# Placing the large on-chip arrays at multiples of 512 bytes in a two-layer backbone kernel

## What is computed

```
def sq_relu_mlp(h, w1, w2):
    return jnp.square(jax.nn.relu(h @ w1)) @ w2

for l in range(DEPTH):                       # 2 layers
    mod_x = (jax.nn.silu(c) @ w_mod[l] + b_mod[l])[:, None, :]
    ...
    hx = rms_norm(xs, norm_mix_g[l]) * (1 + sc1) + sh1
    oc, ox = even_mixer(...) if l % 2 == 0 else odd_mixer(...)
    xs = xs + g1 * ox
    xs = xs + g2 * sq_relu_mlp(rms_norm(xs, norm_mlp_g[l]) * (1 + sc2) + sh2, mlp_w1[l], mlp_w2[l])
    ...
return rms_norm(xs, final_norm_g)            # (1, 256, 1024)
```

## The kernel before, in words

| array | before | after |
|---|---|---|
| `cst` (constants: `ident`, `ones`, masks) | 128 (`le` and behind: 160) | the same |
| `vec` | 288 | 288 |
| `cs` | 128 | 128 |
| `xT`, `raw`, `w_hi`, `w_lo` | 128 | 0 |
| `w_hi2`, `w_lo2`, `late_w` | 64 | 0 |
| all of `F`: `h_*`, `hid_*`, `mix_*`, `att_*`, `qkv`, `first_w`, `d_*` | 64 | 0 |
| row k of `up_hi`, `up_lo` | 64 (k + 1) | 64 k |

## Time and profile before

### The profile page before, as it was taken

The page is one execution under the profiler, slowest core; times in us unless marked ns, Lnnn a source line. Parts: engine busy times, 40 slices in busy tenths (PEclk is TensorE's granted clock), DMA queues, the critical chain, the costliest instruction groups (busy, mean ns, idle before and its releaser), DMA issues.

```text
span 1369.7 us, 28118 instructions
## 1 busy us (share of the span) xinstructions
PE 1344.8 (98%) x11256; PEld 1269.9 (93%) x11256; DVE 854.4 (62%) x1308; ACT 701.6 (51%) x1135; POOL 287.9 (21%) x296
## 2 busy tenths in 40 slices
PE   6999999999999999999999999999999999999998
PEld 4899998988899999999999999999998988999998
DVE  4755789985455665543587666566736666765563
ACT  4468888878544455422533322333226665663553
POOL 2000224223566786621100000000020000200002
PEclk9999999999999999999999999999999999999999
DMA  9732232322401110123466565565423320656562
GB/s 327 201 87 85 79 92 78 94 78 77 139 33 34 61 33 32 63 78 101 139 193 193 184 194 190 185 192 182 134 93 123 98 74 32 192 175 204 173 194 78
DMA packets 138030, 170.88 MB, mean 125 GB/s; under 512 B 10912, under 2 KB 121760, under 8 KB 137920
## 3 DMA queue, kind: packets, MB, share of 16 engines
q1 hardware_dynamic: 137312, 169.13, 39.4%
q0 software_dynamic: 608, 0.19, 0.1%
HBM read 168.25 MB, written 1.05 MB: 124 GB/s over the span
## 4 chain that ended last, share of the span: by engine, by line
PE 84%; DVE 7%; ACT 4%; issue 2%; POOL 2%; DMA 1%; SPq 0%; DVEq 0%; ACTq 0%; POOLq 0%
PE bank L2531 54%; PE bank L2538 7%; PE bank L2945 3%; PE bank L2933 3%; DVE qkv L1721 2%; DVE w_lo L1655 2%; PE bank L2457 1%; PE bank L2962 1%; POOL qkv L768 1%; PE bank L3184 1%; PE bank L2887 1%; PE bank L3207 1%; PE bank L2911 1%; PE bank L2809 1%; DMA first_w<-in_w_mod 1%
## 5 line engine op out<-in xcount | busy, mean ns | idle before, releaser
L1655 DVE TENSOR_TENSOR w_lo<-raw,w_hi 128x1024 fp32r<-128x1024 f32 x214 | 267.3, 1250 | 308.9 <-ACT w_hi L915 308.4
L915 ACT ACTIVATE w_hi<-raw 128x1024 fp32r<-128x1024 f32 x214 | 225.5, 1055 | 378.0 <-PE bank L2531 376.0
L2531 PE MATMUL bank<-h_hi,w_hi 128*128 128x256 f32 x1472 | 300.0, 282 | 7.4 <-DVE w_lo L1655 4.9
L2531 PE MATMUL bank<-h_hi,w_lo 128*128 128x256 f32 x1472 | 292.8, 277 | 0.0
L2531 PE MATMUL bank<-h_lo,w_hi 128*128 128x256 f32 x1472 | 287.5, 278 | 0.0
L2531 PEld LDWEIGHTS bank<-h_hi,w_hi 128*128 128x128 f32 x1472 | 225.5, 188 | 18.1 <-issue 10.2
L2531 PEld LDWEIGHTS bank<-h_hi,w_lo 128*128 128x128 f32 x1472 | 225.1, 188 | 0.0
L2531 PEld LDWEIGHTS bank<-h_lo,w_hi 128*128 128x128 f32 x1472 | 222.0, 188 | 0.3 <-DVE h_lo L1914 0.2
L2531 PE MATMUL bank<-hid_hi,w_hi 128*128 128x256 f32 x768 | 173.5, 280 | 0.0
L2531 PE MATMUL bank<-hid_hi,w_lo 128*128 128x256 f32 x768 | 172.2, 278 | 0.0
L2531 PE MATMUL bank<-hid_lo,w_hi 128*128 128x256 f32 x768 | 172.2, 278 | 0.0
(11 more groups left out here) (363 smaller groups left out, 2484.7 us busy)
## 6 DMA issues: line engine op xcount, KB each, us to landing
raw<-in_mlp_w SPq DMA_DIRECT2D x128, 512.0 KB, 3.7
late_w<-in_w_mod SPq DMA_DIRECT2D x56, 512.0 KB, 4.4
raw<-in_even_w_in SPq DMA_DIRECT2D x48, 512.0 KB, 3.7
raw<-in_w_mod SPq DMA_DIRECT2D x24, 512.0 KB, 4.4
first_w<-in_w_mod SPq DMA_DIRECT2D x16, 512.0 KB, 10.8
raw<-in_even_w_out SPq DMA_DIRECT2D x16, 512.0 KB, 3.5
raw<-in_attn_w_qkv SPq DMA_DIRECT2D x16, 512.0 KB, 3.7
raw<-in_attn_w_o SPq DMA_DIRECT2D x8, 512.0 KB, 3.5
```

Of the source, the lines that this page charges most:

```text
L915: act.activation(stored(w_hi, j, four), raw[:, j % RAW], ACT.Copy).then_inc(hi_ready, 1)
L1655: dve.tensor_tensor(stored(w_lo, j, four), raw[:, j % RAW], stored(w_hi, j, four).bitcast(F32), ALU.subtract).then_inc(split_done, 1)
L2531: return pe.matmul(bank[2 * pair + t][:, c - n0:c - n0 + CTX], w_[:, k, t * P:(t + 1) * P], x_[:, c:c + CTX], start=(kk == 0 and first and ...
```

## The change

The small arrays (`modv` to `gate_bias`) are placed ahead of the large ones, the next address is rounded up to a multiple of 512, and then the large arrays follow, all of which have sizes that are multiples of 512. `d_last` (16 elements) goes into columns of `sp_x` that nothing else uses. No instruction is added, removed or moved in order; what changes is the address in each. The large arrays from `mod_off` on lie 64 bytes lower, `xT`, `raw`, `w_hi` and `w_lo` 4,992 bytes higher.

```
--- before.py
+++ after.py
@@ -136,6 +136,7 @@
 LRU_TILES = 8
 
 
+ALIGNED = 512
 SHIFT, UP_ROW = 2, 272
 
 
@@ -205,10 +206,6 @@
 
         mod_row = at("mod_row", (nc.sbuf_base + 31) // 32 * 32 + 4 * N_EARLY, [2 * UNIT_C])
         vec = place("vec", [NVEC])
-        xT = place("xT", [KT, T])
-        raw = place("raw", [RAW, UNIT_K, UNIT_C])
-        w_hi = place("w_hi", [SPLIT, UNIT_K, UNIT_C], F32R)
-        w_lo = place("w_lo", [SPLIT, UNIT_K, UNIT_C], F32R)
         modv = place("modv", [2, 6, 8, 2])
         gain = place("gain", [2, 2, 8, 2])
         cs = place("cs", [8, 32])
@@ -228,9 +225,14 @@
         gate_bias = place("gate_bias", [2, 16])
         lru_c = sp_x[:, 64:80]
         lru_h = vec[:, VEC["lam"]:VEC["lam"] + 16]
-        d_last = place("d_last", [2, 2, 4])
+        d_last = sp_x[:, 32:48].rearrange("p (t d c) -> p t d c", t=2, d=2)
         beta_gap = sp_x[:, 0:32].rearrange("p (n h) -> p n h", h=8)
         beta_p = sp_p[:, 0:64].rearrange("p (s d h) -> p s d h", d=2, h=8)
+        base[0] = (base[0] + ALIGNED - 1) // ALIGNED * ALIGNED
+        xT = place("xT", [KT, T])
+        raw = place("raw", [RAW, UNIT_K, UNIT_C])
+        w_hi = place("w_hi", [SPLIT, UNIT_K, UNIT_C], F32R)
+        w_lo = place("w_lo", [SPLIT, UNIT_K, UNIT_C], F32R)
         mod_off = base[0]
         base[0] += 16384
         w_hi2 = at("w_hi2", mod_off, [SPLIT, UNIT_K, UNIT_C], F32R)
```

More of the change, by code:

```diff
@@ L207, in build @@
         vec = place("vec", [NVEC])
[L208 to L211, removed]
         modv = place("modv", [2, 6, 8, 2])
```

## The result

The changed kernel takes 1406.64 us (median of 5 runs, 1405.79 to 1407.12), the kernel before 1371.89 us beside it (median of 5, 1368.95 to 1373.92). The ratio is 1.0251, 95% interval 1.0240 to 1.0262: slower by 2.5%. The profiled executions have spans of 1405.1 us after and 1369.7 us before, a difference of 35.4 us.

What follows compares the result with a forecast made beforehand. TensorE, busy 98% of the span, was taken as the bound. 42 us of slower matmuls less 6 us hidden gave +36 on 1370.0, so 1406 us, range 1380 to 1414.

Steps and rivals of the forecast that it cites:

- The pace: 256-column fp32r matmuls of line 2531: with equal remainders they run at 120 ns instead of 113 or 118.
- One sign: Span of the first MLP and its neighbours: to grow by 5.9%.
- The argument for it: Second MLP's up projection: row times of 0.72 or 0.74 us follow the difference of the operands' remainders, not one remainder.
- The 17 units at a distance of 0: Units with equal remainders in the earlier trace, 408 matmuls: all run at 120 ns.
- The cost in TensorE time: Line 2531: 39 us from 5,869 matmuls and 3 us from 1,068, together 42 us.
- The hidden part: Waits of TensorE in qkv bodies and six more holes: they absorb 6 us of the slowing, bounds 0 and 10.
- The second up projection: Line 2538, 768 matmuls of 258 columns: moving remainders walk over all eight places before and after, so 0.
- fp32 matmuls and transposes: Delta rule and attention matmuls keep difference 0: 0; transposes against ident taken as 0, between -2 and +2 us.
- DMA: Weight loads into SBUF: taken as 0, with 3.0 us of wait on the first weights as bound for gain or loss.
- (a): Rival: operands' own remainders decide and 0 is best, 113.3 ns everywhere, 1356 us; chance 0.07.
- (b): Rival: address doesn't matter, the steps come from what else runs; 1370 us, within 0.2%; chance 0.07.
- (c): Rival: layer 0 tiles that meet two moving blocks settle at 117.8 ns; 1391 us; chance 0.08.

Runs made afterwards that it cites:

- The first run: The changed kernel with every large array, weights and moving operands alike, 64 bytes higher, difference still 0: 1408.52 us.
- the sweep: Changed kernel with w_hi and w_lo at remainder 0, everything behind them 64 to 448 bytes higher (steps of 64, also 160 and 224): 1372.5 to 1407.0 us.
- the last two runs: Changed kernel with all weight slots at remainder 0, moving operands at 192: 1370.55 us; the same with up_hi and up_lo rows of 1,280 bytes: 1369.15 us.

## Why the prediction was right, and where its steps were not

Forecast 1406 us, measured 1406.64; range 1380 to 1414. That the two agree within 1 us is in part luck: the forecast was 36 on top of 1370.0, and measured is 34.8 on top of 1371.9, so that an increase put 1 us too high stands on a start put 2 us too low.

**The pace.** Right: 7,376 of the matmuls run at 120 ns. The first run (all 64 higher) and the sweep together show that it is the distance. At 448 with other remainders the mean pace is again 116.7 ns, so no part of the remainders themselves shows. One sign was given too high: the first MLP and its neighbours were to grow by 5.9%, the ratio of 120 to 113.3. A unit did, but from the first MLP to the last of layer 1's projections it was 20.7 us in 434.3, 4.8%, as some units were at 118 before and transposes and waits lie between.

**The argument for it.** Right in its conclusion, weaker than it looked. I read the up projection's rows as a scale of eight distances. In the kernel after, whose weight slots have one remainder, units of rows 0 to 3 and of rows 4 to 7 have the same four row times (720, 714, 726 and 740 ns): there are four distances, modulo 256. Before, 0 and 256 had had two times, 732 and 720, so a row's time does not hang on its distance alone. And a unit takes 2.90 us at any of them, so row times tell that places matter, but not how much for 256 columns; the order that they gave for 192 was the reverse of the true one. The 17 units at a distance of 0, on which the size rested, were what carried it. (The 117.8 ns of the earlier trace rows are right, but not from the figures beside them: 1.42 us over 12 is 118.3; the trace has 1.413 us.)

**The cost in TensorE time.** Predicted 42 us. Over all 7,680, up to whatever instruction follows, the start-to-start times add up to 898.6 us before and 934.9 after, 36.3 us more, in which the holes have already shrunk: what the longer ones hold beyond 120 ns went from 18.8 to 13.9 us. Pace alone is 36.3 + 4.9 = 41.2 us. Right.

**The hidden part.** Predicted 6 us, bounds 0 and 10. 41.2 - 35.4 = 5.8 us in the span; the holes of line 2533 account for 4.9. A qkv body, between the first matmuls of two groups of the recurrence's gates, before:

```profile
206.74 1.99 PE L2768 MATMUL bank<-xc,lru_w 64*128 64x512 f32 x8
...
231.70 1.56 PE L2768 MATMUL bank<-xc,lru_w 64*128 64x512 f32 x6
```

and after:

```profile
212.55 1.99 PE L2770 MATMUL bank<-xc,lru_w 64*128 64x512 f32 x8
...
237.87 1.99 PE L2770 MATMUL bank<-xc,lru_w 64*128 64x512 f32 x8
```

24.96 and 25.32 us: of 192 x 6.7 ns = 1.28 us a body shows 0.36 and hides 0.92, a little more than the 0.75 that I had read off two places. (The second line before counts 6 of the group's 8 matmuls.) After the change all six bodies from 111 to 263 us take 25.32 us. Before, they took 24.07 twice, then 24.79, 24.83 and 24.97 twice: the first two, from 109 to 157 us, hide next to nothing and show 1.25, the next two hide 0.75 and 0.79. The chain of waits of the kernel after, 200 to 260 us, where the earlier trace rows run through three other engines:

```profile
by line: PE bank L2533 92.6%; PE bank L2770 6.4%; PE bank L2518 1.2%
```

No other engine is left in the chain: TensorE sets the pace there too, and further slowing should show whole, which no run tried.

**Terms put at 0.** The second up projection: 2.90 us a unit, right. fp32 matmuls and transposes: their groups have the same start-to-start times in all traces (111.6 ns for 128 columns, 109 for most transposes). For transposes against `ident`, which stays in place, that holds at every distance of the sweep. Most fp32 matmuls are between arrays that move together and stay at a distance of 0; only the last two runs put some 192 apart (`d_r` and `d_vn` in the delta rule), and those kept 111.6. DMA: `raw` from `w_mod` lands in 4.2 us after against 4.4, the spread of all these runs, and TensorE stands longer on the first load, not shorter:

```profile
PE bank L2459 <- DMA first_w<-in_w_mod: 3.5, 2, 2.3
```

Half a microsecond against the earlier trace rows, inside the bound, and with a sign that says nothing of the landing: at distance 384, where the median landing of `first_w` was slower (11.3 us against 10.4), the stand was 2.4 us.

**The rivals.** (a), best at 0, fell: at 0 a unit takes 5.76 us and not 5.44. (b), no effect of places, and with it the Trainium skill's rule (SBUF — State Buffer, Who interferes with whom) that TensorE never waits on anyone: the sweep disagrees by up to 34 us, and no other engine's work was changed in it. The rule may hold between engines, which no run here tests; what the runs show is that TensorE's pace hangs on where its own two operands lie. (c), tiles with two moving blocks settling at 117.8, fell: layer 0 runs at 120.0 as layer 1.

Why the distance costs what it costs, that the matmul's moving read and the next weights' load meet in the same part of a partition's memory, is an argument from the pattern. No run looks inside; that the fp32 instructions which were moved apart kept their pace, while fp32r changed its own, stays unexplained.

## What to carry to other kernels

Round numbers for addresses are not safe: two operands that TensorE reads side by side should be placed by their distance, and equal remainders modulo 256 were the worst choice for fp32r matmuls of 256 columns (120 ns against 113). Where matmuls are back to back, read their start-to-start time in the timeline and ask why the same instruction has several values; weight slots at different remainders are a free experiment already in the trace. Sweep the offset of one array in steps of 64 bytes over 256: here the best value, 192, was the costliest in the rows of the neighbouring shape of 258 columns.

## What the hardware showed that I had not expected

- The pace of fp32r matmuls of 256 columns with a fresh weight tile each depends on the distance modulo 256 bytes: 120.0 ns at 0, 113.3 or 117.8 at 64 and 192, a mix of 115 to 123 at 128, 160 and 224. I had read a circle of 512.
- At one and the same distance of 192 there are two steady states, 113.3 and 117.8 ns, and interruptions switch between them. In the second down projection a unit of distance 0 was followed by the slower one where the other units were at 192 or 448, and by the faster one where they were at 64 or 320. Without such units one half of it ran at 113.3 throughout and the other at 117.8.
- Two more columns (258) give 120.8 ns on average at all distances tried, also where every row was at 192; that is more than the 0.9 ns that two columns would add to 113.3 at the pace of the 256 (113.3 / 256 = 0.44 ns a column).
- The first weights (`first_w`) landed in a median of 10.4 us in the two traces where their remainder is 0 or 256 and in 10.8 to 11.6 in the twelve others. One remainder, 192, gave 10.8, 11.2 and 11.6 in three kernels, so this is a hint and not shown; nothing of it is seen in the time of the kernel.
